# The decode rows' second feed-forward product as four 32-column products in one bank

## The reference, cut to what matters

```
D_MODEL = 1024; SEQ = 2048; DEC_SEQ = 32; D_FF = 4 * D_MODEL
    ...
    u = rmsnorm(x, norm_ffn_pre) @ w_up              # (rows, 4096)
    f = jnp.square(jax.nn.relu(u)) @ w_down          # (rows, 1024)
    x = x + rmsnorm(f, norm_ffn_post)
```

## Time and profile before

| | us |
|---|---|
| median of 3 runs | 3084.81 (3082.12 to 3088.74) |
| profiled execution | 3086.13 |
| its span | 3084.4 |
| TensorE busy | 2897.8 (94%) |
| VectorE busy | 1493.9 (48%) |
| ScalarE busy | 925.3 (30%) |
| GpSimd busy | 286.0 (9%) |
| granted TensorE clock, mean | 0.972 |

### The profile page before, as it was taken

One profiled execution on the slowest core, in us unless ns is written; L12 is line 12 of the kernel. 1 busy time (PEld: TensorE's weight loads), 2 busy tenths in 40 slices (PEclk: granted clock), 3 DMA queues, 4 the chain that ended last, 5 costly groups with the idle time before them and its releaser, 6 DMA issues.

```text
span 3084.4 us, 39331 instructions
## 1 busy us (share of the span) xinstructions
PE 2897.8 (94%) x14977; PEld 2386.1 (77%) x14977; DVE 1493.9 (48%) x3000; ACT 925.3 (30%) x1838; POOL 286.0 (9%) x420
## 2 busy tenths in 40 slices
PE   5999996899978999999699999999989999999997
PEld 4888885677856777766578888888879899898895
DVE  3223332333236877777444454444465444544446
ACT  3222222222125666666322111211132111121112
POOL 0122211111112111110000000000021000000003
PEclk8999998899989999999799999999999999999998
DMA  4111102332432211110321111111133111111112
GB/s 148 35 34 34 34 21 85 129 120 96 145 104 99 80 59 55 56 37 27 115 83 43 54 45 50 41 54 41 41 118 103 55 41 41 41 46 49 41 55 99
DMA packets 105660, 204.63 MB, mean 66 GB/s; under 512 B 11024, under 2 KB 47888, under 8 KB 105552
## 3 DMA queue, kind: packets, MB, share of 16 engines
q1 hardware_dynamic: 103248, 194.79, 19.1%
q0 software_dynamic: 2304, 8.39, 0.8%
HBM read 168.28 MB, written 34.87 MB: 66 GB/s over the span
## 4 chain that ended last, share of the span: by engine, by line
PE 48%; DVE 2%; DMA 0%; ACT 0%; issue 0%; SPq 0%
PE bank L2101 24%; PE bank L2065 23%; DVE ffn_facc L1899 1%; PE bank L2056 0%; DVE ffn_upl L1873 0%; DVE ffn_facc L1940 0%; DVE ffn_hTl L1892 0%; DVE ffn_x L1886 0%; DMA ffn_raw<-in_w_up_dram 0%; DMA ffn_gain_x<-in_norm_ffn_pre_dram 0%; DVE ffn_dnl L1880 0%; DMA ffn_x<-x_scratch 0%; ACT ffn_hTh L1762 0%; ACT ffn_relu L1782 0%; DVE ffn_facc L1906 0%
## 5 line engine op out<-in xcount | busy, mean ns | idle before, releaser
L1940 DVE TENSOR_TENSOR ffn_facc<-bank,ffn_facc 128x512 f32<-128x512 f32 x510 | 346.1, 689 | 243.7 <-PE bank L2101 242.5
L2065 PE MATMUL bank<-ffn_hTh,ffn_uph 128*128 128x352 f32 (+1 forms) x1280 | 451.0, 352 | 8.7 <-DVE ffn_upl L1873 5.5
L2065 PE MATMUL bank<-ffn_hTl,ffn_uph 128*128 128x352 f32 (+1 forms) x1280 | 449.6, 351 | 0.0
L2065 PE MATMUL bank<-ffn_hTh,ffn_upl 128*128 128x352 f32 (+1 forms) x1280 | 449.3, 351 | 0.0
L2101 PE MATMUL bank<-ffn_dnh,ffn_hidh 128*128 128x512 f32 x1088 | 430.3, 396 | 9.4 <-DVE ffn_dnl L1880 6.2
L2101 PE MATMUL bank<-ffn_dnh,ffn_hidl 128*128 128x512 f32 x1088 | 430.9, 396 | 0.0
L2101 PE MATMUL bank<-ffn_dnl,ffn_hidh 128*128 128x512 f32 x1088 | 429.9, 395 | 0.0
L1913 DVE SCALAR_TENSOR_TENSOR ffn_relu<-bank,ffn_relu 128x352 f32<-128x352 f32 (+1 forms) x160 | 94.6, 591 | 484.4 <-ACT ffn_relu L1782 484.2
L2065 PEld LDWEIGHTS bank<-ffn_hTh,ffn_uph 128*128 128x128 f32 x1280 | 241.1, 188 | 33.7 <-issue 7.7
L2065 PEld LDWEIGHTS bank<-ffn_hTl,ffn_uph 128*128 128x128 f32 x1280 | 241.3, 188 | 23.7
L2065 PEld LDWEIGHTS bank<-ffn_hTh,ffn_upl 128*128 128x128 f32 x1280 | 241.0, 188 | 22.6
(11 more groups left out here) (196 smaller groups left out, 4392.3 us busy)
## 6 DMA issues: line engine op xcount, KB each, us to landing
ffn_raw<-in_w_up_dram SPq DMA_DIRECT2D x64, 512.0 KB, 4.4
ffn_raw<-in_w_down_dram SPq DMA_DIRECT2D x64, 512.0 KB, 4.1
ffn_x<-x_scratch SPq DMA_DIRECT2D x24, 512.0 KB, 4.3
retp_x<-in_x_prompt_dram SPq DMA_DIRECT2D x16, 512.0 KB, 3.6
retw_raw<-in_w_in_dram SPq DMA_DIRECT2D x8, 1024.0 KB, 5.1
dpp_x<-in_x_prompt_dram SPq DMA_DIRECT2D x16, 512.0 KB, 4.9
dp_kst<-in_cache_diff_k_dram SPq DMA_DIRECT2D x32, 256.0 KB, 2.9
mix_xr<-in_x_prompt_dram SPq DMA_DIRECT2D x16, 512.0 KB, 3.3
```

Of the source, the lines that this page charges most:

```text
L1940: nc.vector.tensor_tensor(out=part, in0=Dn[i % s.rd][:], in1=part, op=ALU.add).then_inc(s_add, 1)
L2065: last = nc.tensor.matmul(bank[:, 0:w], l[:, k, f * P:(f + 1) * P], r[:, k, c:c + w], start=(k == 0 and q == 0), stop=(k == 7 and q == 2))
```

## The change

The decode tile leaves `down` and `accumulate` (`whole` holds the tiles of 128 rows). ScalarE copies its hidden values unsplit, in f32, to a small buffer `hd`, and `decode_down` multiplies them with the raw weights, in full f32, as four products of 128 x 32 with 512 moving columns: 2 halves x 2 `f`, each in its own 32 partitions of bank `DD` (`U[3]`), gathered there over all 16 groups. It stands behind `down` of the group before (for group 0: behind the third unit of `up` of group 1). SP waits for it before it overwrites the raw buffer. At the end ScalarE copies the bank to SBUF, `decode_sum` adds the strips by two products with a matrix of identities (`pick`), ahead of row tile 2 of group 15, and VectorE copies the sums to `facc` (`decode_row`). The order of finishing in block 1 becomes decode tile, tile 8, ..., tile 15 (`order`, `finished`), and the steps of finishing work on 32 partitions for the decode tile. The padding, its memsets and the wait for them go.

```diff
-        hidden_flat = [[sb(f"hid{n}{u}", [P, FG * tokens + P - dec], F32R) for n in "hl"] for u in range(2)]
+        hidden_flat = [[sb(f"hid{n}{u}", [P, FG * tokens], F32R) for n in "hl"] for u in range(2)]
+        hd = [sb(f"hidden_decode{u}", [P, FG, dec]) for u in range(2)]
+        pick = sb("pick", [P, dec])
...
-                self.downs = [(i, n) for i in range(self.nb) for n in range(2)]
+                self.whole = [i for i in range(self.nb) if rows(self.tiles[i]) == P]
+                self.downs = [(i, n) for i in self.whole for n in range(2)]
+                self.order = [i for i in range(self.nb) if i not in self.whole] + self.whole
...
+        DD = U[3]
...
                     def step(g, e, last, near):                      # SP
+                        if s.b and not last:
+                            sp.wait_ge(s_dq, g + 1)
...
                 def hid_hi(s, g, e, i, units):                       # ScalarE
                     f, c, w = units[i]
                     act.wait_ge(s_h, s.u0 + g * s.ku + i + 1)
+                    if s.b and c + w == tokens:
+                        nc.scalar.activation(hd[e][:, f, :], rh[i % 2][:, w - dec:w], ACT.Copy).then_inc(s_hd, 1)
...
                 act.wait_ge(s_hl, s.u0 + G * s.ku)
-                for i in range(s.nb):
-                    meansq_f(s, i)
+                act.wait_ge(s_dq, G)
+                nc.scalar.activation(rh[0][:], DD[:], ACT.Copy).then_inc(s_dqs, 1)
+                for p in range(s.nb):
+                    meansq_f(s, p)
...
+                def decode_row():                                    # VectorE
+                    for n in range(2):
+                        dve.wait_ge(s_ds, 1)
+                        nc.vector.tensor_copy(facc[0:dec, nb_max - 1, n * N:(n + 1) * N], U[n][0:dec, :]).then_inc(s_dec, 1)
...
-                for i in range(s.nb):
+                for i in s.whole:
                     accumulate(s, G - 1, i)
+                    if i == 1:
+                        decode_row()
                     if i >= 2:
                         norm_f(s, i - 2)
-                norm_f(s, s.nb - 2)
-                norm_f(s, s.nb - 1)
-                for i in range(by_dve, nb_max):
-                    last_residual(i)
+                for p in range(s.nb - 3, s.nb):
+                    norm_f(s, p)
+                for p in range(by_dve, nb_max):
+                    last_residual(p)
...
                         up_unit(U[i % s.ru], unit, range(8)).then_inc(s_u, 1)     # TensorE, up
+                        if s.b and second and i == 2:
+                            decode_down(0, 0)
...
+                        if s.b and ending and tile == 2 and n == 0:               # TensorE, down
+                            decode_sum()
...
+                def decode_down(g, e):
+                    count = 2 * G + 2 * g + 3 - (1 if isinstance(g, int) and g == G - 1 else 0)
+                    pe.wait_ge(s_hd, FG * (g + 1))
+                    for i in range(FG):
+                        pe.wait_ge(s_raw[i], 16 * count)
+                    for n in range(2):
+                        for f in range(FG):
+                            rows_out = slice((FG * n + f) * dec, (FG * n + f + 1) * dec)
+                            last = nc.tensor.matmul(DD[rows_out, :], hd[e][:, f, :], raw[f][:, n * N:(n + 1) * N],
+                                                    start=(isinstance(g, int) and g == 0),
+                                                    stop=(isinstance(g, int) and g == G - 1))
+                    last.then_inc(s_dq, 1)
+
+                def decode_sum():
+                    pe.wait_ge(s_dqs, 1)
+                    pe.wait_ge(s_pick, 1)
+                    for n in range(2):
+                        side = slice(n * P // 2, (n + 1) * P // 2)
+                        last = nc.tensor.matmul(U[n][0:dec, :], pick[side, :], rh[0][side, :], start=True, stop=True)
+                    last.then_inc(s_ds, 1)
...
                         if not last:
                             up(s, g + 1)
                             down(s, g, e)
+                            if s.b:
+                                decode_down(g + 1, 1 - e)
```

More of the change, by code:

```diff
@@ L1595, in hid @@
         def hid(e, part):
-            return hidden_flat[e][part][:, 0:FG * tokens].rearrange("p (f n) -> p f n", f=FG)
+            return hidden_flat[e][part][:].rearrange("p (f n) -> p f n", f=FG)
         class Shape:
@@ L1628, in steps, with finished, residual, store @@
             step(G - 1, 1, True, True)
+        DD = U[3]
+        assert shapes[1].ru == 3 and dec * 4 == P
         by_dve = nb_max - 3
-        def residual(eng, queue, b, i):
+        def finished(b, p):
+            i = shapes[b].order[p]
             t = blocks[b][i]
[L1635 to L1638, removed]
-            else:
[L1640 to L1646, removed]
-            else:
[L1648 to L1651, removed]
+            return i, t, shapes[b].t0 + p
+        def residual(eng, queue, b, p):
+            i, t, c = finished(b, p)
+            if b == 0 and p < 2:
+                eng.wait_ge(s_xT, 2 * (10 + p) + 2)
+            elif b and p - 2 >= by_dve:
+                eng.wait_ge(s_yd, p - 1 - by_dve)
+            else:
+                eng.wait_ge(s_y, c - 1 if p >= 2 else b1[0])
+            queue.dma_start(xe[p % 2][0:rows(t), :], x1v[t][0:rows(t), :]).then_inc(s_xe[b][p % 2], 16)
+        def store(eng, queue, b, p):
+            i, t, c = finished(b, p)
+            if b and p >= by_dve:
+                eng.wait_ge(s_yd, p + 1 - by_dve)
+            else:
+                eng.wait_ge(s_y, c + 1)
+            if p >= 2:
+                eng.wait_ge(s_st[b][p % 2], 16 * (p // 2))
+            queue.dma_start(yv[t] if t < nt else y_s[0], facc[0:rows(t), i, :]).then_inc(s_st[b][p % 2], 16)
         with nc.Block() as block:
@@ L1729, in _ @@
                             pool.wait_ge(s_st[0][u], 16 * (len(b0) // 2))
[L1730 to L1735, removed]
+                    for p in range(2):
+                        rstd_f(s, p)
+                    for p in range(s.nb):
+                        i, t, c = finished(s.b, p)
+                        if p + 2 < s.nb:
+                            rstd_f(s, p + 2)
+                        if s.b and p >= by_dve:
                             continue
-                        pool.wait_ge(s_xe[s.b][i % 2], 16 * (i // 2 + 1))
-                        pool.wait_ge(s_fn, t + 1)
+                        pool.wait_ge(s_xe[s.b][p % 2], 16 * (p // 2 + 1))
+                        pool.wait_ge(s_fn, c + 1)
                         nc.gpsimd.tensor_tensor(out=facc[0:rows(t), i, :], in0=facc[0:rows(t), i, :],
-                                                in1=xe[i % 2][0:rows(t), :], op=ALU.add).then_inc(s_y, 1)
+                                                in1=xe[p % 2][0:rows(t), :], op=ALU.add).then_inc(s_y, 1)
                         if s.b == 0:
-                            store(pool, nc.gpsimd, 0, i)
-                            if i + 2 < s.nb:
-                                residual(pool, nc.gpsimd, 0, i + 2)
+                            store(pool, nc.gpsimd, 0, p)
+                            if p + 2 < s.nb:
+                                residual(pool, nc.gpsimd, 0, p + 2)
             @block.scalar
@@ L1943, in _ @@
                 dve.sem_inc(s_add, 4)
-                for e in range(2):
-                    for part in range(2):
-                        nc.vector.memset(hidden_flat[e][part][:, FG * tokens:].bitcast(F32), 0.0).then_inc(s_pad, 1)
+                nc.vector.tensor_reduce(out=pick[:], in_=ident[:].rearrange("p (j m) -> p m j", m=dec), axis=AX.X,
+                                        op=ALU.add).then_inc(s_pick, 1)
                 dve.wait_ge(s_gain, 16)
@@ L2027, in step @@
                         if not last:
-                            for tile in range(s.nb):
+                            for tile in s.whole:
                                 if tile == 1 and not near:
```

58 lines of the change are left out of this document (34 added, 24 removed).

## The result

The changed kernel takes 3064.23 us (median of 4 runs, 3063.17 to 3064.66), the kernel before 3083.47 in the same comparison; the ratio is 0.9934 with a 95% interval of 0.9917 to 0.9952. The forecast was 3062.5, with a range of 3057 to 3070. The profiled execution took 3064.58 us, its span 3062.8, 21.6 less than before; by the medians the gain is 19.2 us.

What follows compares the result with a forecast made beforehand. TensorE was taken to bound the loop over column groups in block 1. Terms -41.7 + 18.2 + 0.95 = -22.6 us, from the profiled 3086.13 to 3063.5, by the median 3062.2; forecast 3062.5 us, range 3057 to 3070.

Steps and rivals of the forecast that it cites:

- What goes: Block 1, groups 0 to 14: dropping the ninth tile's 12 TensorE products saves 15 x 2.78 = 41.7 us.
- What comes: Each group: four f32 strip products cost 1.21 us a set with the switch; fifteen sets cost 18.2 us.
- rival 3: Strip products over all rows don't lie side by side: 3.6 us a set, +13 us, 3098 us; chance 0.04.
- Rival 1: Each set pays more at its borders: 1.5 us a set, 4.5 us more, 3067 us; chance 0.14.
- Rival 4: Better than thought: 1.0 us a set and no end loss, -27.5 us, 3057 us; chance 0.08.
- The waits: TensorE's set waits for copies and raw weights, SP's weight loads for the set: priced at nothing, once under 3 us if wrong.
- no wait on SP ended by the set in the loop: Sign expected in the profile after: SP's next first-product weight load, waiting for the split too, isn't moved.
- The last group: Group 15 and finishing, not bound by TensorE: sum, add, larger last tile and clock together +0.95 us.
- The clock: Sixteenth set cuts the 3.54 us pause before the last group to about 2.4, so no fall: -1.7 us.
- The add of GpSimd: Last group: decode row first makes tile 1 third in order, its reciprocal root early for GpSimd's first add: -0.7 us.
- The sum: Last group: two products summing the strips ahead of tile 2, with a switch, before the first normalisation: +1.15 us.
- The larger last tile: Kernel end: last tile in order has 128 rows, so its residual load and last store take longer: +2.2 us.

Runs made afterwards that it cites:

- one_strip: Changed kernel with only one of the four strip products run in groups 1 to 14: median 3061.57 us, ratio to before 0.9919.
- same_strip: Changed kernel with all four products writing the same strip of 32 partitions in groups 1 to 14: median 3096.94 us, ratio to before 1.0038.
- narrow: Changed kernel with 128 moving columns instead of 512 in the four products of groups 1 to 14: median 3055.66 us, ratio to before 0.9903.
- row_last: Changed kernel with the finishing order of before, tiles 8 to 15 first and decode row last: median 3061.99 us, ratio to before 0.9925.
- best_again: Changed kernel with the strip sum in the pause before group 15's second product and decode row last, repeated: median 3056.79 us, ratio to before 0.9912.
- after_again: The changed kernel itself, run again beside the best version on the same chip: median 3063.39 us, ratio to before 0.9934.
- after: The changed kernel, first measurement, against the kernel before: median 3064.23 us, ratio 0.9934.

## Why the prediction was right, and where it was not

- **What goes: 41.7 us forecast.** A tile is still 2.78 us (22.24 for eight in the changed kernel). Group 0 lost 0.7 more: its second product went from 25.73 to 22.24 us. Of this, 0.58 is a stop of TensorE behind a copy by VectorE in that group (0.81 us from product to product) that is no longer there. I had said that TensorE didn't need slack there. Whether the ring of 4 banks or the shorter list for VectorE took the wait away was not separated. The stop in the kernel before:

```profile
2343.18 0.39 PE L2101 MATMUL bank<-ffn_dnh,ffn_hidl 128*128 128x512 f32 x1
2343.99 0.50 PE L2101 MATMUL bank<-ffn_dnh,ffn_hidh 128*128 128x512 f32 x1 [0.42 <-DVE ffn_facc L1938]
```

- **What comes: 1.21 us a set forecast, 1.17 measured.** Taking the border from the rows of the decode values and the length from streamed volume was right, and one_strip, same_strip and narrow show why: side by side by strip, 0.85 us of streaming, 0.32 of borders. The upper bound of 3.6 us was that of same_strip (3.73), so rival 3 had its price right and its condition wrong. Rival 1 falls too: the unrolled group and those in the loop take the same time to 0.01 us, so a wait whose value is worked out from the loop's counter adds nothing that shows; no run has the 0.3 us that I allowed for it. Rival 4 was added up wrongly: 1.0 us a set and no end loss make -41.7 + 15 = -26.7, not -27.5. Groups 0 to 14 came to -24.8 instead of -23.5.
- **The waits.** Right in what they cost: no engine waits for SP's later loads, and the set costs nothing in the last pause: group 15's second product starts 3.93 us behind the last of group 14 in both kernels. But my sign, no wait on SP ended by the set in the loop, did not come: SP waits for the set there, up to 17.0 us, and only the split behind it keeps this hidden.
- **The last group: +0.95 forecast, +2.67 measured.** This is the step that failed, by two of its four terms, the clock and the add. The clock (-1.7) was wrong: I took one pause of 2.67 us without a fall for a rule. The pause was cut to 2.55 us, and the clock still fell, a little later (first full for about 1.3 us, then 0.50), as it had in the kernel before: 0 in place of -1.7. Had it stayed full, it would have been worth 1.19 at the end, by one_strip. The add of GpSimd (-0.7) was wrong as well: I had looked at which square it waits for, and not at what stands ahead of that square on ScalarE. With the decode row first, ScalarE's squares of tiles 8 and 9 stand behind one that waits for the sum. The first add came 1.03 us after the first normalisation (3025.97), not sooner than the 0.83 of before: +0.2 in place of -0.7. The sum (+1.15) was right: 1.07 from 3019.74 to 3021.04, less 0.23, and 0.11 more at the product behind it. The larger last tile (+2.2) measured 1.16 for the load and 0.65 for the store by the marks of the two kernels, and 1.16 and 0.64 in row_last. At the first of VectorE's residuals the end was 0.86 us late (39.17 us after the group's start, 38.31 before), and 0.86 + 1.16 + 0.65 is the 2.67. It had been 1.33 late at GpSimd's first add; of the 0.47 won back on the way, 0.31 is a wait of one add for its residual rows in the kernel before, and the rest was not followed up.
- **The total** was right to 1.0 us in the profiled spans (-22.6 and -21.6), but partly by luck: the loop gave 1.3 more and the end 1.7 less than forecast, and the phases ahead added 0.5. The large terms, 41.7 and 18.2, were right by their mechanism; that the misses nearly cancel was not foreseen.

On the clock: of six profiled executions with the pause of 2.55 us ahead of group 15, five had a fall (the changed kernel twice, row_last, same_strip, narrow) and one_strip had none. The five with the sum in the pause had none. So the length of the pause alone doesn't decide it: one and the same pause went both ways. That the sum in the pause keeps the clock up is made likely by five against none, one of the five side by side with a fall (best_again, after_again). Whether it does so by its work or by leaving a shorter stop (1.58 us) was not told apart, and what decides in a pause left empty stays open. In after, after_again and row_last the clock fell about a microsecond into the work, in same_strip and narrow it was low there from the start.

## What to carry to other kernels

A tile that is mostly padding is cheaper as narrow products in separate output strips of one bank, even in full f32, as long as each product has a strip of its own. Here four in four strips cost 1.17 us, four in one strip 3.73, and the padding 2.78. A set in the same trace with the same streamed volume and full-width products on both sides gave the price, borders included (1.21 us forecast). And when an item is moved to the front of a finishing chain, look at what each in-order engine then holds behind it: here the dependence on the late sum cost what the order should have won, and putting the sum into a pause and the smallest tile last gave 4.5 us more at the end of the kernel, 1.2 to 1.6 of them because the clock no longer fell.

## What the runs showed of the hardware

- Two records and eight in four strips take the same time (1.04 and 1.06 us), over all 128 rows and 512 columns, and eight in one strip 3.62 us. The Trainium skill ("TensorE: Matmul & The Clock Gate", section "Part 3: Packing small matmuls — row/col tiling") says that a load runs beside products only when its row group differs; these sets do not agree, since all share the rows and six more loads of 0.108 us cost 0.02. In same_strip not even the strip differs, and the second load still lies beside the first record. The Trainium skill does not speak against packing in that section, as my prediction put it: it offers packing by rows and by columns for small products, and only the sentence on the loads stood against this one.
- An add by GpSimd over 32 partitions and 1024 columns takes as long as over 128 (2.40 us, 3027.00 and 3030.86), and VectorE's residual too (1.21 us in row_last, 1.22 here): a tile of 32 rows is no cheaper to finish, except in its DMAs (in the kernel before 128 KB land in 3.1 us, 512 KB in 4.3).
- After a pause the clock may first be full and fall a good microsecond into the work: from 3013.74 to 3017.74 its mean was 0.57, while the microsecond before, the first of the work, had 1.00.
